# Values of three attentions: zero-padded 128-column weights replaced by two 64-column halves of TensorE

## The chip, the cores and the metric

The kernel runs on one core of a Trainium2 chip. The metric is the device time of one execution in microseconds (us). TensorE multiplies, VectorE (DVE) and ScalarE (ACT) do the softmax and carry results out of PSUM, SyncE (SP) issues the weight transfers, GpSimd (POOL) some small ones. In the profile PE is TensorE's matmul side and PEld its weight loads. TensorE's clock is granted at one of two levels, 1.2 GHz (0.50 in the profile) or 2.4 GHz (1.00).

## The reference

Four layers on 256 tokens of width 1024, all in float32. The first two layers are a gated linear attention with a spatial gating unit, a cross attention and a mixture of 16 experts. The last two layers ("e", even, and "o", odd) are what the change touches:

```
layer e: nsa attention, 8 heads of 64 columns, 3 branches each (compressed keys, all keys, window)
         moba attention, 8 heads of 64 columns
layer o: mla attention, 4 heads of 128 columns
         swa attention, 8 heads of 64 columns
each head:  s = q k^T * scale + bias ;  p = softmax(s) ;  o = p v
then:       x = x + gate * (concat(o) @ w_out) ;  then 16 experts
```

The values v of a head are 64 columns wide, except in mla, where they are 128 wide.

## The kernel before

Each engine runs one program in order, and the engines meet on semaphores. Results of TensorE go to one of eight PSUM banks; a bank has a job, a count of "full" and a count of "drained". Weights arrive by DMA in a ring of slots in SBUF, and a slot is given back when TensorE has used it, so the transfers follow TensorE.

The 64-column heads are taken in pairs: heads i and i+4 (a = 0 and a = 1) share a 128x128 tile. A unit of `pair_units` is one pair i, one block T of 128 queries and one branch. Its output is transposed, with 128 rows in PSUM: rows 0 to 63 belong to a = 0, rows 64 to 127 to a = 1. In SBUF, the values of side a lie in a block of 128 columns in which GpSimd has set the other 64 columns to zero (`nv`, `vcz`, `mv`, `swv`). The value step of a unit multiplies each block, zeros included, as a 128-column stationary operand with the transposed probabilities (128 moving columns), and adds both sides a and all key tiles kt into the same 128 rows. A key tile is 128 keys (15 for the compressed branch), and a unit has one key tile, or two for T = 1 in the branches with all keys. So a unit has 2 or 4 value matmuls. In float32 a matmul is two MATMUL records and two LDWEIGHTS records in the trace: 4 or 8 records for a unit.

The order in `attention` is a software pipeline over units, written out by hand. In step k TensorE does the scores of unit k, the transposes of the probabilities of unit k-3 (line 799, name ".t"), and the values of unit k-4 (lines 928 to 934). ScalarE in step k carries the transposes of unit k-3 into `aPT` and takes the exponentials of unit k. VectorE in step k adds the bias and takes the maximum of unit k (line 1943), normalises unit k-1 (lines 1963 and 1801) and copies the output of unit k-4 into `oT` (line 1979), after the last branch of a pair. After the last unit TensorE waits for all outputs and starts `project_rows` (the product with w_out), and the expert stage follows.

Layer e has 24 nsa units and then 8 moba units; layer o has 4 mla units and then 8 swa units. `mm`, the helper at line 767, issues each matmul; all products have that line. In the expert stage `gate_up` and `down` call it with 64 stationary columns for each side of the bank (`o[cols, :]`), two sides in turn.

Of the kernel before, what the change touches and what calls it, by code (L numbers as in the profile page):

```python
# [28 lines left out]
P = 128  # L29
# [31 lines left out]
DH = 64  # L61
# [241 lines left out]
def program(nc, weights, ada, cst, prm, vecs, x_in, xT_in, memT_in, out, scratch):  # L303
    ctx = ExitStack()
    with ctx:
# [100 lines left out]
        def aP(u):  # L406

            i = u["n"] % 4
            if i < 2:
                return aP2[:, i, :, :]  # L410
            if i == 3:
                return cut(work, 2048, 2, S) if u["name"][1] == "." else xT[:, 0:2, :]
            return cut(work, EX + 3072 if u["name"][1] == "." else 12672, 2, S)
# [175 lines left out]
        def pair_units(tag, q, branches, chunk0):  # L589

            out = []
            for i in range(PAIRS):
                for T in range(NT):
                    t = slice(T * P, (T + 1) * P)
                    for b, (kf, vf, n, g, biases, sink) in enumerate(branches):
                        nk_ = n or (T + 1) * P
                        tiles = 1 if n else T + 1
                        out.append(dict(
                            name=f"{tag}.{i}.{T}.{b}", nk=nk_, tiles=tiles, kp=min(nk_, P),
                            bias=biases(i, T), sink=sink and sink(i, T),  # L600
                            gate=None if g is None else g(i, T),
                            scores=[[(q[:, i, t], kf(i, a)[:, 0:nk_])] for a in range(2)],
                            pv=[(0, a, kt, vf(i, a, kt)) for a in range(2) for kt in range(tiles)],
                            first=b == 0, last=b == len(branches) - 1, o=f"{tag}.o.{i}.{T}",
                            regions=1, dest=oT[:, chunk0 + i:chunk0 + i + 1, t]))
            return out
# [15 lines left out]
        def nsa_units():  # L622
            return pair_units("nsa", nq, [
                (lambda i, a: kcz[:, a, :], lambda i, a, kt: vcz[0:N_CMP, a, :], N_CMP, nsa_gate(0), cmp_bias, None),
                (lambda i, a: nk[0][:, a, :], lambda i, a, kt: nv[0][:, kt, a, :], None, nsa_gate(1), causal_bias, None),
                (lambda i, a: nk[1][:, a, :], lambda i, a, kt: nv[1][:, kt, a, :], None, nsa_gate(2), causal_bias,
                 before(0)),
            ], 0)

        def moba_units():  # L630
            return pair_units("moba", mq, [
                (lambda i, a: mk[:, i + 4 * a, :], lambda i, a, kt: mv[:, kt, i + 4 * a, :], None, None, causal_bias,
                 None),
            ], 4)

        def swa_units():
            return pair_units("swa", swq, [
                (lambda i, a: swk[:, a, :], lambda i, a, kt: swv[:, kt, a, :], None, None, causal_bias,
                 before(1)),
            ], 4)  # L640
# [100 lines left out]
        def _(pe):  # L741
# [24 lines left out]
            def mm(o, lhsT, rhs, start, stop):  # L766
                ins = nc.tensor.matmul(o, lhsT, rhs, start=start, stop=stop)  # L767
                if release[0] and not stop:
                    ins.then_inc(halves_done, release[0])
                    release[0] = 0  # L770
                return ins

            def begin(name):
                if name not in banks.jobs:
                    banks.add(name)
                banks.wait_free(pe, name)
                return psum[banks.jobs[name][0]]

            def end(name, ins):
                ins.then_inc(banks.full[banks.jobs[name][0]], 1)  # L780

            def ready(name):
                banks.wait_drained(pe, name)

            def product(name, parts, fresh=None):

                bank = begin(name)
                for n, (c0, c1, rows, pairs) in enumerate(parts):
                    for k, (a, b) in enumerate(pairs):
                        if fresh and n == 0 and k % 6 == 0:  # L790
                            ready(f"{fresh}.{k // 6}")
                        ins = mm(bank[0:rows, c0:c1], a, b, k == 0, k == len(pairs) - 1)
                end(name, ins)

            def transposes(name, pairs):
                bank = begin(name)
                for c0, c1, rows, src in pairs:
                    k = src.shape[0]
                    ins = nc.tensor.transpose(bank[0:rows, c0:c1], src, ident[0:k, 0:k])  # L799
                end(name, ins)  # L800
# [104 lines left out]
            def attention(units, between=None, before_values=None):  # L905
                n = len(units)
                for k in range(n + 4):
                    if k < n:
                        u = units[k]
                        product(u["name"] + ".s", [(a * S, a * S + u["nk"], P, u["scores"][a]) for a in range(2)])  # L910
                    if k == 2 and between:
                        between()
                    if 3 <= k <= n + 2:
                        u = units[k - 3]
                        pe.wait_ge(att_prob, u["n"] + 1)
                        src = aP(u)
                        transposes(u["name"] + ".t", [
                            ((2 * a + kt) * P, (2 * a + kt + 1) * P, u["kp"], src[:, a, kt * P:kt * P + u["kp"]])
                            for a in range(2) for kt in range(u["tiles"])])
                    if k == 4 and before_values:  # L920
                        before_values()
                    if k >= 4:
                        u = units[k - 4]
                        if u["first"]:
                            begin(u["o"])
                        bank = psum[banks.jobs[u["o"]][0]]
                        ready(u["name"] + ".t")
                        src = aPT[:, u["n"] % 2, :, :]
                        for j, (r, a, kt, v) in enumerate(u["pv"]):
                            fresh = u["first"] and (j == 0 or u["pv"][j - 1][0] != r)  # L930
                            done = u["last"] and (j == len(u["pv"]) - 1 or u["pv"][j + 1][0] != r)
                            ins = mm(bank[:, r * P:(r + 1) * P], v, src[0:u["kp"], 2 * a + kt, :], fresh, done)
                        if u["last"]:
                            end(u["o"], ins)

# [207 lines left out]
            def first_layer(l):  # L1143
# [91 lines left out]

                us = numbered(cross_units(f"{tg}.x"), ATT[f"{tg}.x"])
                attention(us, lambda: memory_values(1), values_ready)
                project_rows3(f"{tg}.xo", us)
                if l == 0:
# [74 lines left out]
            for n in ("e.q.0", "e.q.1", "e.ks", "e.kw", "e.vs", "e.vw", "e.kc", "e.vc",  # L1314
                      "e.mq.0", "e.mq.1", "e.mk.0", "e.mk.1", "e.mv.0", "e.mv.1"):
                ready(n)
            attention(numbered(nsa_units(), ATT["nsa"]) + numbered(moba_units(), ATT["moba"]))
            for i in range(PAIRS):
                for T in range(NT):
# [47 lines left out]
            for n in ("o.sq.0", "o.sq.1", "o.sk", "o.sv"):  # L1367
                ready(n)
            attention(numbered(mla_units(), ATT["mla"]) + numbered(swa_units(), ATT["swa"]))
            for i in range(PAIRS):  # L1370
                for T in range(NT):
# [1473 lines left out]
```

## Time and profile before

| | |
|---|---|
| median of 3 runs | 1863.09 us (1862.43, 1863.09, 2954.26) |
| the profiled execution | 1866.2 us |
| its span, first to last instruction | 1864.4 us |
| mean granted clock of TensorE | 0.96 |
| PE busy | 1694.4 us, 91% of the span |
| DVE busy | 761.8 us, 41% |
| ACT busy | 398.7 us, 21% |

The third run is far off the other two and plays no part below. Shares are means over stages that have different limits: the two attention stages, near 1092 to 1155 us and 1520 to 1554 us of the span, are read by themselves. A busy PE record includes the time in which its result still travels, so records overlap; the distance from the start of one group to the start of the next is what they cost.

### The profile page before, as it was taken

To read this page: it belongs to the slowest core of one execution; us is meant where nothing else is said; L and a number is where in the kernel's file an instruction comes from. 1 tells how busy PE (TensorE), PEld (TensorE's weight loads), DVE (VectorE), ACT (ScalarE), POOL (GpSimd) and SP (SyncE) were. 2 spreads that over 40 slices of the span, in tenths; PEclk is the share of its full clock that TensorE was granted. 3 is DMA by queue.
4 is the path that set the end of the run, shared out by engine and by line. 5 is a ranking of instruction groups with operands and counts; after the bars stand their busy time and mean duration, and the time that the engine had idled before them with its cause. 6 is when DMAs were issued, how large, how long until landed. Compare 5 with 4: busy or idle time off the path is not lost.

```text
span 1864.4 us, 20556 instructions
## 1 busy us (share of the span) xinstructions
PE 1694.4 (91%) x8053; PEld 982.3 (53%) x8053; DVE 761.8 (41%) x1621; ACT 398.7 (21%) x761; POOL 92.8 (5%) x144
## 2 busy tenths in 40 slices
PE   8999989999799998899886999799998788799995
PEld 5587754343456776444335876444443564454342
DVE  1678742221356766222116356532221644512223
ACT  1232321111022232111103355011110341111111
POOL 1111100000110110000001000000000100000000
PEclk9999979999899999899997999799999899799998
DMA  9868599999974875799996521497999741679995
GB/s 380 343 236 323 226 330 410 421 421 421 420 295 149 321 272 215 316 422 421 421 423 255 194 78 67 182 360 284 423 421 423 277 181 67 263 291 383 421 422 240
DMA packets 83739, 578.84 MB, mean 310 GB/s; under 512 B 8896, under 2 KB 13232, under 8 KB 28336
## 3 DMA queue, kind: packets, MB, share of 16 engines
q1 hardware_dynamic: 60624, 500.20, 66.2%
q0 software_dynamic: 16416, 63.97, 9.1%
q10 hardware_dynamic: 6592, 13.20, 2.1%
q8 instruction: 73, 1.20, 0.3%
q14 instruction: 34, 0.28, 0.0%
HBM read 574.13 MB, written 3.20 MB: 310 GB/s over the span
## 4 chain that ended last, share of the span: by engine, by line
PE 73%; DMA 15%; DVE 7%; ACT 2%; issue 2%; SPq 0%; POOL 0%; POOLq 0%; DVEq 0%; ACTq 0%
PE bank L767 70%; DMA ring<-in_weights 12%; DMA hi_ring<-in_weights 2%; PE bank L799 2%; DVE mix L1943 1%; DVE work L1801 1%; ACT work L1388 1%; DMA consts<-in_cst 1%; ACT mix L1388 1%; DVE mix L1801 1%; DVE small L1801 1%; PE bank L895 0%; DVE oT L1979 0%; DVE x L1801 0%; DVE small L1952 0%
## 5 line engine op out<-in xcount | busy, mean ns | idle before, releaser
L767 PE MATMUL bank<-ring,work 128*64 128x512 f32 (+2 forms) x1516 | 390.5, 584 | 23.7 <-DMA ring<-in_weights 22.3
L1388 ACT ACTIVATE work<-bank 128x512 f32<-128x512 f32 (+6 forms) x234 | 123.4, 531 | 831.6 <-PE bank L767 427.1
L767 PEld LDWEIGHTS bank<-ring,work 128*64 128x64 f32 (+2 forms) x1516 | 141.4, 144 | 252.7 <-issue 243.4
L767 PE MATMUL bank<-ring,oT 128*64 128x512 f32 (+1 forms) x864 | 221.2, 596 | 11.0 <-DMA ring<-in_weights 9.0
L1801 DVE TENSOR_TENSOR work_parts<-bank,work_parts 128x512 fp32r<-128x512 f32 x68 | 47.0, 692 | 370.6 <-ACT work_parts L1388 370.6
L767 PE MATMUL bank<-work_parts 128*128 128x256 f32 (+2 forms) x612 | 151.5, 357 | 21.6 <-DVE work_parts L2029 18.9
L767 PE MATMUL bank<-hi_ring,work 128*64 128x512 f32 (+1 forms) x608 | 154.3, 596 | 7.5 <-DMA hi_ring<-in_weights 6.0
L767 PEld LDWEIGHTS bank<-ring,oT 128*64 128x64 f32 (+1 forms) x864 | 76.1, 144 | 137.4 <-issue 136.8
L767 PEld LDWEIGHTS bank<-work_parts 128*128 128x128 f32 x612 | 108.2, 205 | 70.5 <-issue 37.8
L2118 DVE SCALAR_TENSOR_TENSOR work<-bank,small,work 128x512 f32<-128x512 f32 x34 | 25.5, 751 | 282.7 <-PE bank L767 213.6
L767 PE MATMUL bank<-ring,xT 128*128 128x512 f32 (+2 forms) x352 | 139.0, 554 | 1.7 <-DVE xT L2261 1.7
L767 PE MATMUL bank<-work 128*128 128x128 f32 (+3 forms) x600 | 97.6, 310 | 13.9 <-ACT work L1388 11.4
L1801 DVE TENSOR_TENSOR ring_parts<-ring,hi_ring_parts 128x2048 fp32r<-128x2048 f32 x38 | 85.3, 2287 | 54.3 <-ACT hi_ring_parts L1388 54.3
L1388 ACT ACTIVATE work_parts<-bank 128x512 fp32r<-128x512 f32 (+1 forms) x88 | 51.3, 583 | 258.4 <-PE bank L767 213.4
L767 PEld LDWEIGHTS bank<-ring,xT 128*128 128x128 f32 x352 | 67.2, 192 | 69.6 <-issue 67.5
L767 PEld LDWEIGHTS bank<-hi_ring,work 128*64 128x64 f32 (+1 forms) x608 | 52.2, 144 | 95.1 <-issue 93.2
L767 PEld LDWEIGHTS bank<-work 128*128 128x128 f32 (+1 forms) x600 | 82.9, 198 | 25.9 <-issue 15.0
L767 PE MATMUL bank<-hi_ring,oT 128*64 128x512 f32 x416 | 94.2, 597 | 2.4 <-DMA hi_ring<-in_weights 2.4
L2580 POOL TENSOR_TENSOR small<-small,consts 128x1 f32<-128x1 f32 (+3 forms) x22 | 22.8, 1037 | 1253.9 <-DVE small L1809 1253.9
L1388 ACT ACTIVATE hi_ring_parts<-ring 128x2048 fp32r<-128x2048 f32 x38 | 70.4, 1902 | 42.1 <-PE bank L767 29.7
L767 PE MATMUL bank<-oT_parts,hi_ring_parts 128*128 128x256 f32 x264 | 75.3, 285 | 0.0
L767 PE MATMUL bank<-hi_ring_parts,oT_parts 128*128 128x512 f32 (+1 forms) x192 | 69.9, 364 | 0.6 <-DVE xT_parts L1801 0.6
(236 smaller groups left out, 2052.2 us busy)
## 6 DMA issues: line engine op xcount, KB each, us to landing
ring<-in_weights SPq DMA_DIRECT2D x244, 1024.0 KB, 15.2
hi_ring<-in_weights SPq DMA_DIRECT2D x118, 1024.0 KB, 16.0
ring<-in_weights SPq DMA_DIRECT2D x52, 2048.0 KB, 10.5
hi_ring<-in_ada POOLq DMA_DIRECT2D x38, 512.0 KB, 11.8
mod_rows<-in_ada POOLq DMA_DIRECT2D x25, 512.0 KB, 6.1
work<-in_ada POOLq DMA_DIRECT2D x22, 512.0 KB, 6.1
hi_ring<-in_weights SPq DMA_DIRECT2D x5, 2048.0 KB, 10.6
work<-in_vecs POOLq DMA_DIRECT2D x8, 1024.0 KB, 7.5
```

Of the source, the lines that this page charges most:

```text
L767: ins = nc.tensor.matmul(o, lhsT, rhs, start=start, stop=stop)
L799: ins = nc.tensor.transpose(bank[0:rows, c0:c1], src, ident[0:k, 0:k])
L1388: return nc.scalar.activation(o, i, f, **kw)
L1801: return v.tensor_tensor(o, a, b, op)
L1943: ins = v.tensor_tensor_reduce(out=aS[:, i, a, 0:nk_], in0=p_[:, a * S:a * S + nk_], in1=u["bias"][a], scale=1.0, scalar=LOW, op0=ALU.add, ...
L2118: v.scalar_tensor_tensor(out=eh[:, r % 2, :], in0=p_[:, :], scalar=slot_gate[:, home:home + 1], in1=esig[:, r % 2, :], op0=ALU.mult, op1=A ...
L2580: nc.gpsimd.tensor_tensor(stat_out[:, at:at + n], stat_in[:, at:at + n], cs("half")[:, 0:n], ALU.pow) \
```

## The change

`pair_units` hands over only the 64 columns of values that are not zero, and orders the products of a unit by key tile and then by side. In `attention`, a product with 64 value columns writes only the 64 rows of its side, and each side has its own first and last product. mla and the cross attentions keep 128 columns. The probabilities, the bank, the number of matmuls and the semaphores stay as they are, and so do the zeroed buffers.

```
-    pv=[(0, a, kt, vf(i, a, kt)) for a in range(2) for kt in range(tiles)],
+    pv=[(0, a, kt, vf(i, a, kt)[:, a * DH:(a + 1) * DH]) for kt in range(tiles) for a in range(2)],
...
     for j, (r, a, kt, v) in enumerate(u["pv"]):
-        fresh = u["first"] and (j == 0 or u["pv"][j - 1][0] != r)
-        done = u["last"] and (j == len(u["pv"]) - 1 or u["pv"][j + 1][0] != r)
-        ins = mm(bank[:, r * P:(r + 1) * P], v, src[0:u["kp"], 2 * a + kt, :], fresh, done)
+        rows, sums = slice(0, P), [j_ for j_, of in enumerate(u["pv"]) if of[0] == r]
+        if v.shape[-1] == DH:
+            rows, sums = slice(a * DH, (a + 1) * DH), [j_ for j_ in sums if u["pv"][j_][1] == a]
+        ins = mm(bank[rows, r * P:(r + 1) * P], v, src[0:u["kp"], 2 * a + kt, :],
+                 u["first"] and j == sums[0], u["last"] and j == sums[-1])
```

## Rows read from the trace of the kernel before

**Rows 1.** The page of the profile: engines, and the chain that ended last.

```profile
PE 1694.4 (91%) x8053; PEld 982.3 (53%) x8053; DVE 761.8 (41%) x1621; ACT 398.7 (21%) x761; POOL 92.8 (5%) x144
...
PE 73%; DMA 15%; DVE 7%; ACT 2%; issue 2%; SPq 0%; POOL 0%; POOLq 0%; DVEq 0%; ACTq 0%
```

**Rows 2.** The chain inside layer e's attention: start, duration, what.

```profile
1106.85 0.50 ACT mix L1388 x2
...
1114.51 0.04 DVE xT L1801
1114.55 0.57 issue
1115.12 0.29 DVE oT L1979
```

**Rows 3.** Who waited for whom, 1103 to 1148 us.

```profile
ACT mix L1388 <- DVE small L1952: 4.3, 5, 1.1
...
PE bank L767 <- DVE oT L1979: 2.0, 4, 0.6
```

**Rows 4.** The chain at the end of layer e's attention.

```profile
1151.36 1.13 PE bank L767 x8
...
1152.96 0.61 ACT work L1388
...
1153.70 1.14 PE bank L767 x8
...
1154.94 0.30 DVE oT L1979
```

**Rows 5.** The chain over the whole span.

```profile
1155.59 27.72 PE bank L767 x64
...
1395.30 20.98 DMA ring<-in_weights
...
1548.21 1.53 PE bank L767 x8
1549.74 0.85 PE bank L799 x4
1550.60 2.32 PE bank L767 x12
```

**Rows 6.** Timeline of PE at the end of layer e's attention.

```profile
1152.33 0.60 PE L799 MATMUL bank<-consts,xT 128*128 128x128 f32 x4
1152.76 0.61 PE L767 MATMUL bank<-work 128*128 128x128 f32 x4
```

**Rows 7.** Timeline of PE in an expert stage with 64-column products.

```profile
1361.16 10.52 PE L767 MATMUL bank<-ring,work 128*64 128x512 f32 x48
1371.61 0.50 PE L767 MATMUL bank<-work_parts 128*128 128x256 f32 x2
```

**Rows 8.** Timeline of PE, 128-column transposes between 64-column products.

```profile
1679.51 3.65 PE L767 MATMUL bank<-ring,oT 128*64 128x512 f32 x16
1683.09 0.66 PE L799 MATMUL bank<-consts,work 128*128 128x128 f32 x4
1683.68 3.65 PE L767 MATMUL bank<-ring,oT 128*64 128x512 f32 x16
```

**Rows 9.** Timeline of PE, transposes and then 15-row value products.

```profile
1130.81 0.38 PE L799 MATMUL bank<-consts,xT 128*128 128x128 f32 x2
1131.12 1.12 PE L767 MATMUL bank<-work 15*128 15x128 f32 x5
```

**Rows 10.** Windows: length, busy of PE, PEld, DVE, ACT, POOL, clock, DMA.

```profile
1149.40:1152.80 3.40, 2.12 (x18) 1.73 (x17) 2.02 (x8) 1.96 (x6) 0.00 (x0) 1.00 0.35 123
...
1545.40:1548.70 3.30, 1.27 (x10) 0.88 (x9) 2.37 (x13) 2.17 (x7) 0.00 (x0) 1.00 0.00 0
1548.80:1552.10 3.30, 3.30 (x16) 3.11 (x16) 0.76 (x3) 0.60 (x1) 0.00 (x0) 0.50 0.00 0
```

## The prediction

> **What bounds the kernel now.** I read the page first, then the chain of waits in each attention stage, then who waited for whom, and last the timeline of TensorE. The page says PE: 91% busy and 73% of the chain [rows 1]. That holds for projections and experts, which are most of the span. It does not hold where the change is made. Inside layer e's attention the chain goes back and forth between DVE and ACT and names no PE from 1103 to 1151 us; a piece of it stands here [rows 2]. The reader is to see two things there. The 0.57 us of "issue" ahead of the copy into oT is no wait for the value products: it begins 0.04 us into DVE's own multiplication, which is still running, and the copy follows at once. And ACT's exponentials are steps of the chain. The list of waits says the same: ACT waited for DVE, the one wait that PE has of any size is for DVE (2.0 us in 45), and DVE waited for nobody [rows 3]. So in the body of an attention TensorE is ahead, and a shorter value step buys nothing there.
>
> It is different at the end. When no scores are left, the pipeline empties through TensorE: values of the third last unit (8 records), transposes of the last, ACT's copy, values of the last unit (8 records), DVE's copy, projection [rows 4, 6]. Layer o ends in the same way [rows 5]. These four value steps are what the change can shorten on the path. What is saved there reaches the end: the projection starts on those outputs [rows 5], slots of the ring are given back by TensorE's matmuls, and the transfers that the chain shows later, as the one at 1395.30 us, are issued on slots that come back earlier by the same amount.
>
> **The change, part by part.**
>
> *The width of the products.* Of the 40 units of 64-column heads, 16 have 8 records, 16 have 4 records with 128 rows of keys, and 8 have 4 records with 15 rows: 224 records, before and after. Before, one with 128 stationary and 128 moving columns takes 0.11 us from start to start: 4 take from 1152.33 to 1152.76, 0.108 each, as transposes [rows 6], and the 8 value records from 1151.36 to 1152.33 take 0.97, which is 8 times 0.112 and 0.07 for starting from idle [rows 4, 6]. With 64 columns a side, the trace has such pairs only with 512 moving columns: 24 pairs from 1361.16 to 1371.61 [rows 7], 8 pairs from 1679.51 to 1683.09 [rows 8]. The difference, 16 pairs in 10.45 - 3.58 = 6.87 us, is 0.429 a pair. A full-width record with 512 columns takes 27.72 / 64 = 0.433 [rows 5]. So two 64-column records of different sides run in the time of one, weight loads included. With 128 moving columns I take 0.112 a pair. The bounds are 0.107 (0.429 / 4) and 0.224 (no overlap at all). An 8-record step then saves 4 x 0.112 = 0.45 us and a 4-record step 0.22 us.
>
> *Going from 128 columns to 64 and back.* This is new: each unit now leaves the 128-column form of scores and transposes for its values and returns. The price is in the expert stage. 8 pairs should take 8 x 0.429 = 3.43 and take 3.58: 0.15 too much. The four transposes between them take 0.59 (1683.09 to 1683.68) where four take 0.43 [rows 6, 8]: 0.16 too much. Together 0.30 us for there and back. Bounds: 0.20 (if half of it hides behind short records) and 0.40 (if a return to full-width scores, whose weights take longer to load than the identity's, costs more). The 15-row units pay such a price already: two transposes and then the first 15-row record are 0.31 apart, not 0.22 [rows 9]. For them nothing is added.
>
> The Trainium skill has this rule in its page "TensorEngine Tiling (Array Packing)", section "Key Properties": changing the tiling mode, as against changing the tile, drains the engine. It speaks against this change and gives no figure. The trace agrees with it, by the 0.30 us above; if the drain were free, each of the four end steps would come out 0.15 us better at most.
>
> *The body.* For PE: 16 x (0.45 - 0.30) = +2.4 saved, 16 x (0.22 - 0.30) = -1.3 lost, 8 x 0.22 = +1.8 saved, 2.9 us less in all. With 0.40 for the change of form it is 16 x 0.05 - 16 x 0.18 + 1.8 = -0.3, a wash. Either way it lies beside DVE's work and counts zero. If this cover were gone, 3 us would be the whole of it. No unit gets longer by more than 0.2 us, and PE idles more than that for DVE every few units [rows 3].
>
> *End of layer e, at clock 1.00.* Third last unit: 0.97 becomes 4 x 0.112 plus 0.07 to start, plus 0.05 for the first pair, plus 0.15 for the return to the transposes = 0.72; saves 0.25. ACT's copy and the second last unit's values keep their places (0.43 us of values now lie beside 0.61 of ACT [rows 4, 6]). Last unit: starts from idle, 8 x 0.112 becomes 4 x 0.112 + 0.05; saves 0.40. Nothing is paid for the way back, as PE waits for DVE's copy anyway. Sum 0.65 us.
>
> *End of layer o.* The clock is at 0.50 from 1548.8 to 1552.1 [rows 10]: the four transposes take 0.85 there, 0.21 each [rows 5]. The third last unit's step in the chain is 1.53 there and 1.13 in layer e, where 0.97 of it pass before the transposes start [rows 4 to 6]: so some 1.37 here, part of it at the low clock. It becomes 0.57 at the high clock, and then the transposes wait for the last probabilities, so I count 0.6. The last unit, 8 records of which five stand in the low stretch, saves some 0.35. Together 0.95; bounds 0.6 and 1.6.
>
> *Order of the products, two sums in one bank, the same semaphore on the last product.* No cost. DVE's copy needs both sides and the last record tells of both. No DMA and no wait is added, and nothing is moved past a queue.
>
> **Sum.** 0.65 + 0.95 = 1.6 us. The profiled execution took 1866.2 and would take 1864.6. The median of the runs shown is 3.1 us lower, for reasons that do not lie in these stages as far as I can see, so I take the 1.6 from the median: 1863.1 - 1.6 = 1861.5 us.
>
> **The rivals.**
>
> *The clock falls at the ends, and the time is longer than before.* In layer o, PE was busy 1.27 of 3.30 us, then the clock went to 0.50; in layer e it was busy 2.12 of 3.40 us and the clock stayed at 1.00 [rows 10]. The change takes some 0.45 + 0.22 of these 2.12 away, which leaves 1.5 in 3.4, between the two. If the clock falls there, at 1152.8, for as long as in layer o (3.3 us), the last values cost 0.45 more and the projection runs at half speed up to 1156.1, 0.6 more; if it stays low once more as long, 1.7 more. In layer o the low stretch, which now ends at 1552.1, ahead of the projection, can last on into it: 1.2 to 1.4 us. In the body PE would do in 3.3 us what takes 1.7 and catch up in its idle time; I put 0 to 1 us on each of two falls. Sum 2 to 6, say 3.6 us, against the 1.6 gained: 1865.1 us. For it: each step that is thinned out lies in a stretch that is thin already. Against: in the body PE is busy with scores and transposes in most stretches, and at a low clock the same work makes it busier. It decides from the point at which the low stretches cover more than some 3 us of projection or values.
>
> The rule of the skill's page "TensorE: Matmul & The Clock Gate", Part 1, is that "the default state is throttled, and activity releases the throttle". By this rule a faster value step pays with the clock. The low stretch in layer o agrees with it, and that PE's thinner stretches in the body keep 1.00 speaks for the forecast.
>
> *The halves do not run side by side with 128 moving columns (the change does not do what it says).* Then the values take as long as before and there and back is added, 0.15 to 0.3 on each end step that is followed by transposes, 0.05 on the others: +0.9 us, 1864.0 us. The body would grow by 0.30 a unit, 32 x 0.30 = 10 us of PE in 90, and still fit for the most part. Against it: 0.429 a pair.
>
> *The 1.6 us go nowhere*: a wait behind the projection (a transfer of POOL, the row of gates) takes them up: 1863.1 us. Against it: the chain goes from the projection through PE with no such step.
>
> **How the numbers follow.** Forecast 0.50, clock 0.30, no overlap 0.08, taken up 0.12. The likeliest is 1861.5. Its own range is 1860.5 to 1862.5 by the bounds of the terms, and runs of one kernel lie up to 3 us apart (1862.4 to 1866.2). The range from 1858.5 to 1868 holds the forecast with that scatter and the clock case up to its upper bound, less what lies beyond. 2% is 37 us, about what a measurement of this kernel can tell from no change. All cases lie within 6 us, so "within 2%" gets 0.97; 0.01 and 0.02 are left for faster and slower.
>
> **What would show it.** Value products read as 128*64 (15*64 in the compressed branch), 224 records, pairs 0.11 us apart. The body of each attention lasts as long as before, with PE idle more. From the 8 records of the third last unit to the projection, layer e takes 4.23 us now (1151.36 to 1155.59) and should take 3.6. The clock in the windows at both ends tells the first rival. If pairs start 0.2 us apart, it is the second. I am wrong in kind if DVE or ACT turns out to wait for PE in the body (a gain or a loss of some us there), or if the clock falls several times in it.

## The result, and the profile after

The changed kernel took 1868.36 us (median of 19 runs, 1864.32 to 1872.26) beside 1864.74 us for the kernel before in the same runs. The ratio is 1.0023, with a 95% interval from 1.0017 to 1.0030: slower by about 4 us, within 2%, and on the other side than forecast. The profiled execution took 1872.26 us, the longest of the 19. The page of the changed kernel, against [rows 1]:

```profile
span 1870.5 us, 20556 instructions
...
PE 1695.0 (91%) x8053; PEld 971.1 (52%) x8053; DVE 762.3 (41%) x1621; ACT 399.0 (21%) x761; POOL 93.0 (5%) x144
...
PE 73%; DMA 15%; DVE 7%; issue 2%; ACT 2%; SPq 0%; POOL 0%; POOLq 0%; DVEq 0%; ACTq 0%
```

Nothing shows here: the shares are those of before. The stages tell more. First the products themselves, in the timeline of PE of the changed kernel in layer e's attention:

```profile
1132.41 1.72 PE L767 MATMUL bank<-work 128*64 128x128 f32 x12
1133.96 0.38 PE L799 MATMUL bank<-consts,xT 128*128 128x128 f32 x2
1134.28 0.43 PE L767 MATMUL bank<-work 15*64 15x128 f32 x4
...
1135.97 0.38 PE L799 MATMUL bank<-consts,mix 128*128 128x128 f32 x2
1136.28 1.08 PE L767 MATMUL bank<-work 128*64 128x128 f32 x8
1137.20 0.38 PE L799 MATMUL bank<-consts,mix 128*15 128x128 f32 x2
```

The form is 128*64 and 15*64. The last stretch, from 1136.28 to 1137.20, is four value records and four of scores (the view leaves out that the scores have 128 columns). Two pairs at 0.11, four scores at 0.112 and 0.25 us more make its 0.92 us. The two transposes ahead of it take 0.31 (1135.97 to 1136.28) in place of 0.22, another 0.09. The form there and back costs 0.34 us here, where 0.30 was forecast. The end of layer e's attention, in the chain:

```profile
1154.79 0.66 PE bank L767 x8
...
1156.82 0.67 PE bank L767 x8
...
1158.23 4.10 PE bank L767 x9
```

From the third last unit's values to the projection it is 3.44 us now and was 4.23 [rows 4, 5]: 0.79 us gained. So halves and forms cost about what they should. The loss is in the body of the same attention. The chain of the changed kernel there:

```profile
1102.53 0.29 DVE oT L1981
1102.87 0.92 PE bank L767 x4
1103.78 0.85 PE bank L799 x4
1104.63 2.02 PE bank L767 x12
...
1107.08 3.07 PE bank L767 x12
1110.28 0.42 DVE mix L1945
...
1116.08 0.29 DVE oT L1981
```

A pair of heads in nsa, from one copy into oT to the one of the next pair, took 11.08 us (1104.04, the copy before the one of [rows 2], to 1115.12). Here it takes 13.55, and some 7 us of its chain are PE, which the chain before did not name. The transposes, four in 0.85 us, show why: 0.21 each is the low clock. Windows of the changed kernel (busy of PE, PEld, DVE, ACT, POOL, then the clock), and the list of waits from 1101 to 1151 us:

```profile
1104.00:1108.00 4.00, 4.00 (x25) 2.66 (x24) 2.96 (x20) 3.28 (x14) 0.00 (x0) 0.50 0.01 4
1108.00:1112.00 4.00, 4.00 (x20) 2.80 (x18) 2.05 (x11) 1.18 (x5) 0.00 (x0) 0.74 0.01 2
...
1116.00:1120.00 4.00, 3.58 (x21) 2.92 (x22) 3.20 (x20) 2.83 (x11) 0.00 (x0) 0.61 0.00 0
1120.00:1124.00 4.00, 4.00 (x19) 2.53 (x20) 1.88 (x11) 1.25 (x7) 0.00 (x0) 0.54 0.02 4
...
1128.00:1132.00 4.00, 3.06 (x28) 2.27 (x28) 3.58 (x21) 2.95 (x14) 0.00 (x0) 1.00 0.00 0
```

```profile
ACT work L1390 <- PE bank L799: 5.4, 4, 2.3
DVE mix L1945 <- PE bank L767: 4.8, 4, 1.8
```

Twice the clock went to 0.50 for several microseconds, TensorE was busy nearly all the time, and DVE and ACT waited for it, which they never did before [rows 3]. The busy share does not foretell the second fall: from 1112 to 1116 us, just ahead of it, PE was busy 3.27 of 4 us, and in the same window of the kernel before, which kept 1.00, it was busy 3.03. Layer o's end, in the chain over the whole span, and the window in which its projection starts:

```profile
1552.28 1.12 PE bank L767 x8
...
1555.23 1.14 PE bank L767 x8
...
1557.54 29.25 PE bank L767 x64
```

```profile
1556.00:1560.00 4.00, 2.82 (x7) 1.17 (x4) 0.29 (x1) 0.00 (x0) 0.00 (x0) 0.50 0.00 0
```

The projection's 64 records took 29.25 us, where layer e's of before took 27.72 [rows 5]: 1.5 us for starting at the low clock. The two profiled executions differ by 6.1 us: -1.5 before the first copy of nsa, +4.9 in nsa's first two pairs, -0.8 at layer e's end, +1.4 up to layer o's first copy (a low stretch that lies elsewhere in the mla units), -0.6 at layer o's end, and +2.7 from its projection on, of which 1.5 in the projection and 1.0 in a longer wait for a transfer.

### The profile page after: what moved, and what is told of

Read it like the earlier page. It is cut to its first block, busy times and chain, and to the rows that moved or that the text cites. A ratio compares the mean times of both kernels' runs of the same rounds, so it can differ in the third digit from the quotient of the medians.

```text
span 1870.5 us, 20556 instructions
## 1 busy us (share of the span) xinstructions
PE 1695.0 (91%) x8053; PEld 971.1 (52%) x8053; DVE 762.3 (41%) x1621; ACT 399.0 (21%) x761; POOL 93.0 (5%) x144
## 4 chain that ended last, share of the span: by engine, by line
PE 73%; DMA 15%; DVE 7%; issue 2%; ACT 2%; SPq 0%; POOL 0%; POOLq 0%; DVEq 0%; ACTq 0%
PE bank L767 71%; DMA ring<-in_weights 11%; DMA hi_ring<-in_weights 3%; PE bank L799 2%; DVE work L1803 1%; DVE mix L1945 1%; ACT work L1390 1%; DMA consts<-in_cst 1%; ACT mix L1390 1%; DVE mix L1803 1%; DVE small L1803 0%; PE bank L895 0%; DVE x L1803 0%; DVE oT L1981 0%; ACT xT L1390 0%
## 5 line engine op out<-in xcount | busy, mean ns | idle before, releaser
L767 PE MATMUL bank<-work 128*128 128x128 f32 (+4 forms) x600 | 94.6, 332 | 15.4 <-ACT work L1390 11.9
L767 PEld LDWEIGHTS bank<-work 128*128 128x128 f32 (+2 forms) x600 | 71.2, 186 | 36.4 <-issue 23.8
```

## The experiments

Theory 1: thinner work lets TensorE's clock fall, and at 1.2 GHz TensorE is the bound. Theory 2: the change of form between 64 and 128 columns costs the time, at any clock. Each kernel was timed in turn with the kernel before; these are the ratios. The last column is the granted clock as a mean over a whole execution, median of a kernel's executions; for the kernel before it is 0.962.

| kernel | ratio to before | 95% interval | mean clock |
|---|---|---|---|
| the change | 1.0023 | 1.0017 to 1.0030 | 0.957 |
| form_only | 1.0034 | 1.0021 to 1.0047 | 0.960 |
| twins | 1.0013 | 1.0004 to 1.0023 | 0.962 |
| side_order | 1.0028 | 1.0019 to 1.0037 | 0.958 |
| no_nsa | 1.0006 | 0.9996 to 1.0015 | 0.962 |
| tails | 1.0000 | 0.9991 to 1.0009 | 0.961 |
| filled | 0.9998 | 0.9989 to 1.0007 | 0.963 |
| filled_before | 0.9994 | 0.9984 to 1.0005 | 0.965 |
| tails_filled | 0.9987 | 0.9978 to 0.9996 | 0.963 |
| router_only | 0.9964 | 0.9951 to 0.9978 | 0.969 |
| ends_router | 0.9957 | 0.9940 to 0.9973 | 0.968 |

**form_only: the change of form without the thinner work.**

```
+    if j == 0 and u["regions"] == 1 and u["kp"] == P:
+        mm(bank[0:DH, 0:2], v[:, DH:2 * DH], src[:, 0, 0:2], False, False)
```

> The kernel before, with one product of 64 stationary and 2 moving columns added behind the first value product of each 64-column unit with 128 rows of keys (32 units). Its weights are the zero columns, so that it adds nothing. It brings the change of form, there and back, and leaves the full-width value products. Theory 1 (thinner work lets the clock fall, and TensorE at 1.2 GHz becomes the bound): the clock keeps 1.00 in the body of both attentions, as before; 0.30 us for 32 units is 10 us of PE, hidden in the body, and 0.3 to 1 us at the two ends: ratio 1.0000 to 1.0007. Theory 2 (the change of form itself costs the time): at least what the change cost, ratio 1.0020 or more, with DVE waiting for PE at full clock.

Measured 1.0034. Theory 1's ratio was missed and theory 2's met; the clock was as theory 1 has it. The clock, the copies (in the chain) and the waits of this kernel:

```profile
1108.00:1112.00 4.00, 4.00 (x26) 3.39 (x25) 3.06 (x17) 2.53 (x12) 0.00 (x0) 1.00 0.01 2
```

```profile
1104.32 0.29 DVE oT L1981
...
1116.03 0.29 DVE oT L1981
```

```profile
ACT work L1390 <- PE bank L799: 2.6, 4, 0.7
...
DVE mix L1945 <- PE bank L767: 2.3, 8, 0.4
```

At a clock of 1.00 throughout layer e's body, a pair of nsa takes 11.71 us, not 11.08, and DVE and ACT wait for PE. In the trace the added product and the change of form make a unit's values 0.40 us longer: the fourth value record starts 0.625 us after the second, where 0.223 is usual. A pair of nsa has four such units, two in each half. The half that takes 5.03 us takes 5.03 still; the other went from 6.05 to 6.68. So of the 0.8 us added to each half, one half had room for all, and the other for less than 0.2. That is what the prediction had not seen: in that half the body was close to being TensorE's already. But this is not yet the cause of the change's loss, since the change saves columns as well.

**twins: the change with its columns given back.** Each value product has a twin on the zero columns.

```
-    pv=[(0, a, kt, vf(i, a, kt)[:, a * DH:(a + 1) * DH]) for kt in range(tiles) for a in range(2)],
+    pv=[(0, a, kt, vf(i, a, kt)[:, (a + zero) % 2 * DH:((a + zero) % 2 + 1) * DH])
+        for zero in range(2) for kt in range(tiles) for a in range(2)],
```

> The changed kernel, with each 64-column value product followed by a twin whose 64 stationary columns are the zero columns, so that it adds nothing: 448 records in place of 224, the same time on the array as the full-width products had, and the same changes of form as the changed kernel. Theory 1: the clock is back at 1.00 in the body, DVE waits for PE little or not, ratio to before 0.9998 to 1.0010 (0.3 us for each end that is left). Theory 2: the twins make it worse than the change, ratio 1.0025 or more.

Measured 1.0013, between the theories. The profiled execution was the fastest of twelve, 5 us under their median, so its trace may flatter; the mean clock of all twelve, 0.962, is that of the kernel before. No low stretch lies in layer e's body, the pairs of nsa take 11.50 us by the copies, and DVE waits 1.8 us for PE. More work on the array than in the change, the same changes of form, and less time: theory 2 alone says the opposite. The intervals of the two just overlap, so this shows it less well than the fillers (`filled`, below).

**side_order: side by side or one after the other.**

```
-    for kt in range(tiles) for a in range(2)
+    for a in range(2) for kt in range(tiles)
```

> The changed kernel with the value products of a unit ordered by side and then by key tile. Theory 1: if TensorE pairs the sides only when they alternate, the 16 units of 8 records stretch from 0.45 to up to 0.9 us; TensorE is busier, the clock falls less, and the time lies between before and after, ratio 1.0000 to 1.0020. If it pairs them all the same, the time is that of the change, 1.0023. Theory 2: at least 1.0023, more by the longer products.

Measured 1.0028, not to be told from the change. Its groups of eight value and four score records are as long as the change's (1.73 us, against 1.72), and within them the sides start 0.01 us apart, so TensorE pairs the two sides in either order, and the new order in the diff does nothing. Two low stretches lie in the body again, and the pair at full clock takes 11.07.

**after_again and before_again: one more profiled execution of each.**

> The changed kernel once more, one look. Theory 1: one or more low stretches inside layer e's attention again, with steps of the copies near 5.6 and 8 where they lie and 5.04 and 6.05 elsewhere; low at the start of one or both projections. Rival (the low stretches of the first look were an accident of that execution, and the loss lies elsewhere): none in the body.

> The kernel before once more, one look. Theory 1: no low stretch in layer e's attention after its first units; all steps 5.04 and 6.05. Rival: low stretches there too.

The kernel before had no low stretch in the body and pairs of 11.08 us. The changed kernel had low stretches again, from 1104 and around 1128 us. Its copies into oT in the chain:

```profile
1102.89 0.29 DVE oT L1981
1116.43 0.30 DVE oT L1981
...
1127.51 0.29 DVE oT L1981
```

13.54 us for the pair with a low stretch, and 11.08 for the next, at full clock: what the full-width kernel takes. The third pair, with the second low stretch, takes 11.98 in place of 11.17. So at 2.4 GHz the columns saved pay for the changes of form, and the body's loss, 2.5 us for the one fall and 0.8 for the other, is the clock's. Whether they save more than that the 11.08 us cannot tell, as the chain names only DVE and ACT there.

The profiled executions of all kernels agree on when the clock falls in nsa's body. It fell twice in each of the three with bare 64-column values in nsa (the change, after_again, side_order), and in none of the eleven others: the seven with full-width values there and no fillers in the body (before, before_again, tails, no_nsa, tails_filled, router_only, ends_router), form_only, twins, filled and filled_before.

**tails and no_nsa: where the loss lies.** 64 columns in the last three units of each attention, and in moba and swa.

```
+    if u["regions"] == 1 and k - 4 >= n - 3:
+        v = v[:, a * DH:(a + 1) * DH]
```

```
-    vf(i, a, kt)[:, a * DH:(a + 1) * DH]
+    vf(i, a, kt)[:, a * DH:(a + 1) * DH] if tag != "nsa" else vf(i, a, kt)
```

> 64-column value products only in the last three units of each attention, full width in all others. Theory 1: the body of layer e has no low stretch inside; the ends get 0.7 us shorter each at the same clock, but the projection can start at 1.2 GHz, which costs 1.5 to 2 us where it happens: ratio 0.9990 to 1.0008. Theory 2: two or three changes of form only, ratio 0.9990 to 0.9995.

> 64-column values in moba and swa only, full width in the 24 units of nsa. Theory 1: nsa's steps are 5.04 and 6.05 with no low stretch, moba's 1.87 as before; the ends as in the changed kernel, with the projections at 1.2 GHz in some executions: ratio 0.9990 to 1.0008, so that nsa's body holds nearly all of the change's loss. Rival (each unit costs its change of form, wherever it is): half of the loss stays, 1.0010 or more.

1.0000 and 1.0006. In both, nsa's pairs are back at 11.08 and have no low stretch. Without nsa most of the loss is gone, though the interval of no_nsa, up to 1.0015, does not exclude its rival, and its profiled execution was the fastest of twelve. In it the clock is low from 1149 to 1157 us, and layer e's projection takes 29.83 us, not 27.72. What the ends gain goes again in projections that start at the low clock. Layer o in tails:

```profile
1552.00:1556.00 4.00, 3.75 (x5) 1.72 (x6) 0.00 (x0) 0.00 (x0) 0.00 (x0) 0.50 0.23 39
```

**filled and filled_before: the clock alone.** Products of the identity with itself where TensorE stood idle.

```
+    def fill(bank, times, own=True):
+        for _ in range(times):
+            nc.tensor.matmul(bank[:, 256:384], ident, ident, start=own, stop=own)
...
+    fill(bank, filler(u, k - n))      # third last unit 4, last 2, 15-row units 1, swa with T = 1 4
     ready(u["name"] + ".t")
...
+    if u["kp"] < P:
+        fill(bank, 3, False)
+    if k == n + 3 and u["regions"] == 1:
+        fill(begin(("e" if u["name"][0] == "m" else "o") + ".out.0.0"), 3)
```

> The changed kernel, with products of the identity with itself (128x128, into 128 unused columns of the output's bank) in the places where TensorE stood idle: one ahead of and three behind the 15-row values, four ahead of the values of each T=1 unit of swa, four and two ahead of the values of the third last and the last unit of each attention, three ahead of the projection. They add nothing to the output. Theory 1 (the clock fell because the work was thinner, and at 1.2 GHz TensorE is the bound of the body): no low stretch inside layer e's attention after its first units, none over the projections; steps of the copies into oT as before, 5.04 and 6.05 us in each pair of nsa; ratio to before 0.9980 to 0.9995. Rival (what is lost is the change of form, or the order of the work, at full clock too): the steps stay at 5.5 and 7.9, ratio 1.002 or more.

> The kernel before with the same fillers (one ahead of and two behind the 15-row values, the others alike). Control: what fillers alone are worth to full-width values. Theory 1: the body has no low stretch to take away, so 5.04 and 6.05 stay; layer o's low stretch at its end may go, worth up to 1 us: ratio 0.9990 to 1.0000, above the one of the changed kernel with fillers by the 0.8 us at each end. Rival: as far above or below before as the changed kernel with fillers is above or below the change.

0.9998 for the changed kernel with fillers, against 1.0023 without: more work, 4.7 us less time, intervals well apart. Its windows in nsa's body and at the start of layer o's projection:

```profile
1108.00:1112.00 4.00, 4.00 (x33) 3.00 (x33) 3.50 (x19) 2.33 (x10) 0.00 (x0) 1.00 0.01 2
...
1116.00:1120.00 4.00, 4.00 (x38) 2.94 (x36) 3.46 (x24) 3.69 (x16) 0.00 (x0) 1.00 0.02 4
...
1552.00:1556.00 4.00, 4.00 (x11) 1.83 (x10) 0.00 (x0) 0.00 (x0) 0.00 (x0) 1.00 0.60 201
```

The clock is 1.00 in all of them. The rival falls. Its pairs take 11.31 us (5.04 and 6.27), as the fillers are a little too many for the room; these 0.2 us a pair are part of why the ratio is above the 0.9995 that was expected. On the kernel before, nearly the same fillers give 0.9994, not to be told from none (its pairs take 11.63, 0.55 more, and layer o's end gets shorter at the high clock). So what the fillers give the changed kernel, 0.0025, is more than what they give the kernel before, 0.0006, as the clock theory has it; the 4.7 us are those of the body and of the ends together. filled_before was expected above filled; the two can't be told apart.

**tails_filled: the ends only, with the clock held.** The edits of tails, and the fillers of filled without the ones in the body.

> 64-column values in the last three units of each attention only, with the fillers of the two ends only (four and two ahead of the values of the third last and the last unit, three ahead of the projection). Theory 1: body as before; layer o's projection starts at 2.4 GHz, where the kernel without these fillers had 1.2 GHz until 1558; some 1.6 us at the ends and 2 us of projection: ratio 0.9980 to 0.9993. Rival: the fillers only delay the values they precede, 1.0000 or more.

0.9987, faster than the kernel before by 2.4 us and beyond the interval; nsa's pairs take 11.09. Its projection in layer o starts at the high clock:

```profile
1552.00:1556.00 4.00, 4.00 (x11) 1.76 (x10) 0.00 (x0) 0.00 (x0) 0.00 (x0) 1.00 0.85 287
```

**router_only and ends_router: the same in another stage.** Ahead of the rank product of each expert stage TensorE waits 4.4 to 5.1 us for DVE.

```
+    fill(begin(f"{tag}.rank"), 12 if tag[0] in "01" else 10)
     pe.wait_ge(group_ready, layer + 1)
```

> The kernel before with the fillers ahead of the rank product alone. Theory 1: as the pair above, 1 to 3 us in each layer, ratio 0.9940 to 0.9985. Rival: 1.0000.

"The pair above" is ends_router beside tails_filled; a first version of ends_router, expected at 0.9930 to 0.9975, gave no result.

> The kernel with 64-column values in the last three units of each attention and fillers at the two ends, and the fillers ahead of each layer's rank product (12 products of the identity in the first two layers, 10 in the last two). With the rank fillers alone the kernel before came to 0.9964, with the ends alone to 0.9987. Theory 1: both add up, as they lie in different stretches: 0.9951, between 0.9935 and 0.9967. Rival (the one gain is taken up by the other, or by transfers later): 0.9964 or more.

0.9964 for the kernel before with the helper and one line that calls it in each layer. The gather behind the router in layer e, before and in router_only, each as a window that starts some 1.7 us into it and as the chain over the stage:

```profile
1204.00:1208.00 4.00, 4.00 (x22) 4.00 (x22) 0.42 (x1) 0.66 (x2) 0.00 (x0) 0.57 0.02 4
```

```profile
1202.28 13.38 PE bank L767 x64
```

```profile
1198.00:1202.00 4.00, 4.00 (x29) 2.94 (x30) 1.78 (x6) 0.43 (x2) 0.00 (x0) 1.00 0.00 0
```

```profile
1196.41 11.12 PE bank L767 x64
```

The gather takes 2.3 us less. ends_router, with the ends as well, has the lowest ratio, 0.9957, which meets the sum expected, 0.9951, but can't be told from 0.9964.

## Why the prediction was wrong

- **The halves and the price of a change of form** were right: pairs 0.11 us apart, and 0.34 us there and back for 0.30. The net in the body was foretold as 2.9 us of PE or a wash, hidden at full clock; a pair takes 11.08 us with and without. With 0.34, the half of a pair that has no room (two 4-record units and a 15-row unit) comes to 2 x (0.22 - 0.34) + 0.22 = -0.02 us saved, an estimate that fits.
- **The gain at the ends** was right in layer e (0.65 foretold, 0.79 found) and too high in layer o (0.95 against 0.6), as the low clock covered all of that end.
- **"Beside DVE's work and counts zero"** failed: this is the step of the sum that was wrong. The list of waits showed that DVE and ACT did not wait for PE, and from that I took room for 3 us. form_only shows less than 0.2 us of room in one half of each pair, at full clock, and a fall of the clock made a pair up to 2.5 us longer. An engine that nobody waits for may be late by a hair everywhere.
- **The rival of the clock** was the right mechanism with the wrong size and rank. It was put at 0.30, with "0 to 1 us on each of two falls" in the body. A fall cost up to 2.5 us, as there was too little idle time in which to catch up: 4.9 us for two in the first profiled execution, 2.5 and 0.8 in after_again. With that in place of some 1 us, the rival's 2.0 us over the kernel before become 3.5 to 5.9, and 3.6 were measured. The argument against the rival that failed is "in the body PE is busy with scores and transposes in most stretches". It was, and it was not enough once the values took half the time.
- **The base** is no part of the mechanism: the kernel before came to 1864.74 us in the runs of the result, 1.6 above the median from which the forecast was counted. Of the 6.9 us between 1861.5 and 1868.36 these are 1.6; the rest is a gain of 1.6 that became a loss of 3.6. That the time came out only just above the range of 1868 owes something to it: from 1864.74, the same range would have ended at 1869.6, with the forecast no better for it.
- The other two rivals fall: the halves run side by side, and the gain of the ends was not taken up but reversed.
- The Trainium skill's rule that changing the tiling mode drains the engine (page "TensorEngine Tiling (Array Packing)", "Key Properties") holds in this trace, by the 0.34 us above. The Trainium skill's other rule, that activity releases the throttle (page "TensorE: Matmul & The Clock Gate", Part 1), would have given the right sign. The fillers are its plainest case here: useless products, 4.7 us less.

What stays open: in how many executions each fall occurs, and why the same work in the same kernel falls at one pair and not at another. Both profiled executions of the changed kernel had two stretches in the body, and its runs spread over 8 us, where those of the kernel before, the one far-off run aside, spread over 4.6. The 1.4 us up to layer o's first copy may be chance: from layer e's last copy to it the change took 375.5 us and the kernel before 374.1, but twins, whose code is the same there, took 371.7.

## What to carry to other kernels

Work taken off an engine that only just keeps up can cost time if its clock follows its activity; price a fall of the clock at the room that the engine has at the low level, not at its idle time at the high one. Before calling a stage hidden, measure the room by adding work to it: one small product a unit did it here, and it showed that nearly all the room was in one half of a pair. Where TensorE waits a known time for another engine, products of constants into an unused part of a bank hold its clock for what comes next, and they were worth more (0.36% from one call a layer) than the columns saved.

## What was not expected of the hardware

- TensorE ran the two 64-column sides together also when the program gave one side's two products first and then the other's: groups of 12 records, eight of them of values, took 1.73 us in that order and 1.72 in the other.
- A round trip between the forms costs 0.34 us around 64-column values with 128 moving columns, and one around a single product with 2 moving columns costs 0.40, the product included: 32 such tiny products alone made the kernel slower by 0.34%.
- The clock's falls are not the same in all executions: in the first profiled execution nsa's first two pairs took 13.55 us each and the third 11.18; in the second they took 13.54, 11.08 and 11.98.
